# Moving the gate projection's bank evacuation from ScalarE to VectorE, bias included, in a two-block float32 network kernel

## The reference, cut to what matters

```python
h = rms_norm(x, mix_norm)
z = h @ w_in
u, q, k, v, gl = ...                       # pool, attention and gate parts of z
y_pool = multiscale_pool(u, pool_w, pool_scale)
y_attn = moba_attention(rope(norm(q)), rope(norm(k)), v)   # 8 heads, causal softmax
gates = sigmoid(gl + b_gate).reshape(B, S, 2, D)
merged = gates[:, :, 0] * (y_pool @ w_branch_pool) + gates[:, :, 1] * (y_attn @ w_branch_attn)
x = x + merged @ w_out
```

## Time and profile before

| | |
|---|---|
| time, 3 runs | median 1966.62 us (1966.51 to 1966.93) |
| profiled execution: its own time | 1966.62 us |
| its span in the trace | 1964.8 us |
| PE busy | 1953.6 us (99%) |
| DVE busy | 1363.6 us (69%) |
| ACT busy | 1034.5 us (53%) |
| POOL busy | 163.9 us (8%) |
| granted TensorE clock, mean | 0.999 |
| HBM traffic | 183 GB/s over the span |

### The profile page before, as it was taken

How to read it: one execution, slowest core, us unless ns; L and a number is a source line. 1 busy time by engine, 2 the same in 40 slices (tenths; PEclk the granted TensorE clock), 3 DMA queues, 4 the chain that set the end, 5 groups by cost and what they waited for, 6 DMA issues and landing times.

```text
span 1964.8 us, 27601 instructions
## 1 busy us (share of the span) xinstructions
PE 1953.6 (99%) x10534; PEld 1663.7 (85%) x10534; DVE 1363.6 (69%) x1652; ACT 1034.5 (53%) x1201; POOL 163.9 (8%) x152
## 2 busy tenths in 40 slices
PE   9999999999999999999999999999999999999998
PEld 8888978888888889788888978888888978888887
DVE  7666577666676666777666556577888666677887
ACT  6444555544454455655445554356556554456564
POOL 0000130000000003104001201040001301000000
PEclk9999999999999999999999999999999999999999
DMA  8554645455455546456555544564553544555552
GB/s 326 192 183 181 202 142 193 175 189 192 171 193 192 185 159 213 150 180 230 185 190 181 179 174 143 206 249 171 192 192 140 198 177 161 206 211 187 182 187 86
DMA packets 55132, 365.74 MB, mean 186 GB/s; under 512 B 6672, under 2 KB 7952, under 8 KB 12176
## 3 DMA queue, kind: packets, MB, share of 16 engines
q1 hardware_dynamic: 49680, 349.99, 49.9%
q0 software_dynamic: 1472, 9.44, 1.3%
q10 hardware_dynamic: 3904, 5.25, 1.0%
HBM read 359.40 MB, written 1.05 MB: 183 GB/s over the span
## 4 chain that ended last, share of the span: by engine, by line
PE 98%; DVE 1%; ACT 1%; issue 0%; ACTq 0%; POOL 0%; DVEq 0%; POOLq 0%
PE gate_two L1694 13%; PE up_two L1694 12%; PE bank L1624 9%; PE bank L1626 9%; PE bank L1625 9%; PE gate_two L1624 8%; PE gate_two L1626 8%; PE gate_two L1625 8%; PE gate_two L1696 6%; PE up_two L1696 6%; PE bank L1835 1%; PE up_two L1866 1%; PE up_two L1850 1%; PE bank L2127 1%; PE bank L1875 0%; PE gate_two L1636 0%
## 5 line engine op out<-in xcount | busy, mean ns | idle before, releaser
L1019 DVE TENSOR_TENSOR w_lo<-raw,w_hi 128x2048 fp32r<-128x2048 f32 x318 | 736.1, 2316 | 250.2 <-ACT w_hi L569 244.7
L569 ACT ACTIVATE w_hi<-raw 128x2048 fp32r<-128x2048 f32 x322 | 614.3, 1908 | 94.5 <-PE bank L1626 65.8
L1694 PE MATMUL gate_two<-br_parts,w_hi 128*128 128x512 f32 x1056 | 376.5, 399 | 0.1
L1694 PE MATMUL up_two<-br_parts,w_hi 128*128 128x512 f32 x1024 | 364.1, 398 | 0.0
L1696 PE MATMUL gate_two<-br_parts,w_lo 128*128 128x256 f32 x1056 | 296.3, 281 | 0.0
L1696 PE MATMUL up_two<-br_parts,w_lo 128*128 128x256 f32 x1024 | 287.4, 281 | 0.0
L1694 PEld LDWEIGHTS gate_two<-br_parts,w_hi 128*128 128x128 f32 x1056 | 198.4, 188 | 48.8 <-issue 0.8
L1694 PEld LDWEIGHTS up_two<-br_parts,w_hi 128*128 128x128 f32 x1024 | 192.4, 188 | 47.8
L1696 PEld LDWEIGHTS gate_two<-br_parts,w_lo 128*128 128x128 f32 x1056 | 199.4, 189 | 2.3
L1696 PEld LDWEIGHTS up_two<-br_parts,w_lo 128*128 128x128 f32 x1024 | 193.3, 189 | 0.0
L1624 PE MATMUL bank<-w_lo,hid_hi 128*128 128x512 f32 x480 | 188.6, 393 | 0.0
(11 more groups left out here) (274 smaller groups left out, 3010.6 us busy)
## 6 DMA issues: line engine op xcount, KB each, us to landing
raw<-stream SPq DMA_DIRECT2D x328, 1024.0 KB, 4.8
area<-rpb POOLq DMA_DIRECT2D x2, 1536.0 KB, 7.9
area<-rows POOLq DMA_DIRECT2D x3, 1024.0 KB, 5.1
raw<-stream SPq DMA_DIRECT2D x8, 256.0 KB, 7.4
softT<-area ACTq DMA_DIRECT2D x32, 64.0 KB, 5.2
area<-rows POOLq DMA_DIRECT2D x2, 768.0 KB, 4.7
konst<-consts SPq DMA_DIRECT2D x1, 1344.0 KB, 7.7
area<-xT ACTq DMA_DIRECT2D x4, 256.0 KB, 6.8
```

The costliest lines, as they stand in the source:

```text
L569: act.activation(w_hi[:, s, :], raw[:, s, :], ACT.Copy).then_inc(hi_ready[s], 1)
L1019: dve.tensor_tensor(w_lo[:, s, :], raw[:, s, :], w_hi[:, s, :].bitcast(F32), ALU.subtract).then_inc(lo_ready[s], 1)
L1694: pe.matmul(pair[:, f, :, :], w_hi[:, s, at:at + P], parts[:, :, k, :], start=k == 0, stop=False, skip_group_check=True)
```

## The change

ACT no longer empties the gate banks. DVE does it with one `scalar_tensor_tensor` for each bank, `bank * rs + bias row`, eight for each layer (`gated(m, a)`, m = 9, 11, 13, 15). gated(m, 0) is written at the head of DVE's step m, behind a wait for `wide_half`, and gated(m, 1) after the wait for the chunk's end. ACT's eight copies, its waits for `wide_half`, and DVE's four bias instructions are gone, and with them the signals `gate_evac` and `gate_ready`; PE and ACT wait on `mix_scaled` instead, which now counts to 10. The bias rows come in one POOL-issued transfer of 1 MB rather than two. The second edit is on DVE's queue: the `w_lo` split of slot m in steps 7 to 14, which stood in step m + 1 behind that step's scores, is now the last instruction of step m, as in the other steps.

```diff
-                def gate_bias(n):
-                    part = gate_slots[:, 2 * n - 4:2 * n - 2, :] if n >= 2 else merged_tok[:, :, n * 2 * T:(n + 1) * 2 * T]
-                    row = gate_slots[:, n, :] if n < 3 else last_row
-                    dve.wait_ge(gate_rows_in, (layer + 1) * 32)
-                    dve.wait_ge(gate_evac.sem, here.at(gate_evac, 2 * n + 2))
-                    dve.tensor_tensor(part, part, row.unsqueeze(1).broadcast_to([P, TT, 2 * T]), ALU.add
-                                      ).then_inc(gate_ready.sem, 1)
+                def gated(m, a):
+                    gate, half = divmod((m - 9) // 2, 2)
+                    out = gate_slots[:, 2 * half + a, :] if gate else merged_tok[:, a, half * 2 * T:(half + 1) * 2 * T]
+                    dve.scalar_tensor_tensor(out=out, in0=flat(banks[4 + a][:, :, :]), scalar=rs[:, a:a + 1],
+                                             in1=gate_slots[:, (m - 9) // 2, :], op0=ALU.mult, op1=ALU.add
+                                             ).then_inc(mix_scaled.sem, 1)
...
# DVE, loop over m
+                    if m in (9, 11, 13, 15):
+                        dve.wait_ge(gate_rows_in, (layer + 1) * 16)
+                        dve.wait_ge(wide_half.sem, here.at(wide_half, (m - 5) // 2))
+                        gated(m, 0)
...
+                    if m in (9, 11, 13, 15):
+                        gated(m, 1)
...
-                    if 8 <= m < 16:
-                        split_after(here, c - 1)
...
-                    if m in (9, 11, 13, 15):
-                        gate_bias((m - 9) // 2)
-                    if 0 < m < 7 or 15 <= m < MIX1 - 2:
+                    if 0 < m < MIX1 - 2:
                         split_after(here, c)
# ACT, loop over m
-                    if m in (9, 11, 13, 15):
-                        gate_out(m, 1)
...
-                    if m in (8, 10, 12, 14):
-                        act.wait_ge(wide_half.sem, here.at(wide_half, m // 2 - 2))
-                        gate_out(m + 1, 0)
# PE, loop over m
-                    elif m in (10, 12, 14):
-                        pe.wait_ge(gate_evac.sem, here.at(gate_evac, m - 9))
+                    elif 8 <= m < 16:
+                        pe.wait_ge(mix_scaled.sem, here.at(mix_scaled, m - 7))
...
-                                    (lambda: pe.wait_ge(gate_evac.sem, here.at(gate_evac, m - 8))))
+                                    before_second=lambda: pe.wait_ge(mix_scaled.sem, here.at(mix_scaled, m - 6)))
```

More of the change, by code:

```diff
@@ L194, in hybrid_and_neighbourhood_kernel @@
         gate_slots = area3[:, :, :].rearrange("p f t -> p (f t)").rearrange("p (n c) -> p n c", n=HALVES)
-        last_row = area5[:, 6:8, :].rearrange("p f t -> p (f t)")
         gates2_tok, merged_tok = [area[:, :, :].rearrange("p f t -> p (f t)").rearrange("p (a n) -> p a n", a=TT)
@@ L311, in hybrid_and_neighbourhood_kernel @@
         mix_evac = signal("mix_evac", 6, 30)
-        mix_scaled = signal("mix_scaled", 2)
+        mix_scaled = signal("mix_scaled", 10)
         wide_half = signal("wide_half", 5, 9)
@@ L315, in hybrid_and_neighbourhood_kernel @@
         gate_rows_in = sem("gate_rows_in")
-        gate_evac = signal("gate_evac", 2 * HALVES)
-        gate_ready = signal("gate_ready", HALVES)
         branch_evac = signal("branch_evac", 2, 4)
@@ L479, in _ @@
                 pool.wait_ge(qk_ms.sem, here.at(qk_ms, 4))
-                gate_rows = rows1[layer:layer + 1].rearrange("a p n -> (a p) n")
-                pool.dma_start(flat(area3[:, 0:6, :]), gate_rows[:, 0:6 * T]).then_inc(gate_rows_in, 16)
-                pool.dma_start(last_row, gate_rows[:, 6 * T:8 * T]).then_inc(gate_rows_in, 16)
+                pool.dma_start(flat(area3[:, :, :]), rows1[layer:layer + 1].rearrange("a p n -> (a p) n")
+                               ).then_inc(gate_rows_in, 16)
                 pool.wait_ge(konst_in, 16)
@@ L736, in _ @@
                 split_hi(2, here.uses(FFN_CHUNKS + 2))
[L738 to L744, removed]
                 for m in range(MIX1):
@@ L815, in _ @@
                         gates = flat((area2, area3)[m - 15][:, :, :])
-                        act.wait_ge(gate_ready.sem, here.at(gate_ready, 2 * m - 28))
+                        act.wait_ge(mix_scaled.sem, here.at(mix_scaled, 6 + 4 * (m - 15)))
                         for half in range(2):
@@ L1931, in _ @@
                         pe.wait_ge(mix_evac.sem, here.at(mix_evac, m - 1))
-                    elif m == 8:
-                        pe.wait_ge(mix_scaled.sem, here.at(mix_scaled, 1))
-                    elif m in (10, 12, 14):
-                        pe.wait_ge(gate_evac.sem, here.at(gate_evac, m - 9))
+                    elif 8 <= m < 16:
+                        pe.wait_ge(mix_scaled.sem, here.at(mix_scaled, m - 7))
                     elif m == 16:
@@ L1938, in _ @@
                     elif m == 18:
-                        pe.wait_ge(gate_evac.sem, here.at(gate_evac, 8))
+                        pe.wait_ge(mix_scaled.sem, here.at(mix_scaled, 10))
                         pe.wait_ge(att_ready.sem, here.at(att_ready, HALVES))
@@ L1946, in _ @@
                         wide_tokens(c, m % 2, (banks[4], banks[5]), br_hi, br_lo, wide_half,
-                                    before_second=(lambda: pe.wait_ge(mix_scaled.sem, here.at(mix_scaled, 2))) if m == 8 else
-                                    (lambda: pe.wait_ge(gate_evac.sem, here.at(gate_evac, m - 8))))
+                                    before_second=lambda: pe.wait_ge(mix_scaled.sem, here.at(mix_scaled, m - 6)))
                     elif m in (4, 5):
```

## The result

| | before | after |
|---|---|---|
| time, median | 1966.74 us (1966.51 to 1967.97) | 1977.53 us (1974.76 to 1978.88), 5 runs |
| ratio | | 1.0052, 95% interval 1.0038 to 1.0067 |
| span of the profiled execution | 1964.8 us | 1975.9 us |
| granted TensorE clock, mean | 0.999 | 0.998 |

A forecast was written before the change was run, and what follows sets the result against it. PE, busy 1953.6 us, was taken as the bound. First layer 4.3 + 0.3 + 0.5 = 5.1, second 5.0, sum 10.1 us: 1966.62 + 10.1 = 1976.7 us; range 1973.0 to 1980.5, forecast's own 1974.5 to 1979.5.

The forecast's parts named there:

- That PE would wait for DVE at chunks 10, 12 and 14 of each layer: PE's products at these gate chunks wait behind DVE's gate instruction: about 3 to 4 us at 10, 0.3 and 0.5 after.
- not slower: Rival, chance 0.04: freed ACT runs hi(8) ahead, so lo(8) starts by 259 or so and PE never waits; 1966.6 us.
- The chain to chunk 10, without contention: DVE and ACT in one line from lo(7) through gated(9,0): PE waits 3.16 us in the first layer, 3.1 in the second.
- Contention with POOL, +1.1 us in each layer: POOL's sliding sums stretch DVE before chunk 10: +0.5 us for head 1's stat instruction, +0.6 for lo(8).
- the race: lo(7) starts 0.05 us before POOL's instruction and wins the shared ports; were POOL first, 0.6 us more in each layer.
- The second layer's wait: PE's wait before chunk 10 in the second layer: 3.1 us, with POOL's 1.1 it is 4.2.
- The pairs: Chunk 10 to 12 and chunk 12 to 14 in each layer: PE loses 0.3 us, then 0.5 us.
- The loop is closed: DVE does not wait for PE in it: DVE's loop from gated(11,0) to gated(13,0) takes 14.14 us without waiting for PE, against PE's own 13.60.
- The clock, given 0.12: Rival, chance 0.12: the clock falls in the wait before chunk 10, about 2.7 us per slow stretch; 1979.4 to 1982.1 us.
- turn(1) under 1 us: Sign: before chunk 10, PE waits at turn(1) behind the softmax weights for under 1 us, not added to the sum.
- the granted clock leaves 1.00 in the mixing stages: Sign that the forecast is wrong: TensorE's granted clock departs from 1.00 in the mixing stages; no size given.
- What is gained: nothing: Removing ACT's copies, merging the POOL transfer and splitting earlier save zero, as PE waited for none of it.

The follow-up runs named there:

- the repetition: The changed kernel itself, unaltered, run again to compare the others with it on one chip: 1976.5 us, ratio 1.0045.

## Why the prediction was right, and where it was not

- **That PE would wait for DVE at chunks 10, 12 and 14 of each layer: shown.** Six waits in the list, and none when either half of the change is undone, or when the gate instruction stands ahead of lo(8). The forecast's reason for it (both queues in strict order, everything in one line) is what these runs test, and it held. One figure of the rival "not slower" does not come out: "a chain of 8.9 rather than 12.1 us" names no start, and from hi(7) at 253.60 to 264.94 the chain was 11.34. Nothing else uses it.
- **The chain to chunk 10, without contention: right in sum, not in its links.** 9.40 us was worked out and 9.40 measured, twice; in the kernels with added products and in the repetition it is 9.40 or 9.41 in both layers too. Scores to exp was 0.4 too long. It was measured at one head, from the MEMSET at 277.30, and that head's own instructions lie further apart than in other heads, 0.98 us from the first of the scores to the stat instruction in place of 0.67. DVE's timeline of before shows a pause in it; why is not known:

```profile
277.35 0.29 DVE L1161 CUSTOM_DVE_ANT_0 soft<-bank,konst 128x128 f32<-128x128 f32 x1
277.79 0.08 DVE L1161 DVE_READ_ACCUMULATOR2_ANT stat<- 128x1 f32 x1 [0.16 <-issue]
```

- Lo to gated was 0.2 too short (lo(8) took 2.49) and the handover 0.05 should have been about 0.15: the first `gated` takes 0.74 and PE starts 0.88 behind its start. In the sum these cancel.
- **Contention with POOL, +1.1 us in each layer: wrong.** The step that failed took the middle rows of before for the stat instruction and for lo(8). After the change the stat instruction took 0.16 and lo(8) 0.2 more than undisturbed. Both had been stretched by POOL's instructions that stood beside them in the old order; the change moved DVE's instructions against POOL's, so these rows no longer described the neighbours. POOL's timeline beside lo(7) at 256.33:

```profile
256.38 2.82 POOL L489 TENSOR_TENSOR area<-area 128x248 f32<-128x248 f32 x1
```

- Lo(7) began 0.05 us ahead of it, kept its 2.29, and POOL paid: 2.82 for what took 0.72. The turn-taking of the Trainium skill, "SBUF — State Buffer", section "SBUF: two separate sides", agrees in both layers. The prediction had named the race and its outcome, and then added contention further down the chain all the same.
- **The second layer's wait** was shorter, 2.6 against 3.2 us, with the same chain of 9.40: lo(7) started 0.06 us behind chunk 9 there and 0.69 behind it in the first layer, because DVE's first scores began 1.5 us after PE's in the one and 2.7 in the other (1.95 and 2.07 in before). The profiles on record show that this distance varies: 1.2 to 2.7 us over both layers of the ten profiled executions. In the repetition it is 1.36 in the first layer, and lo(7) starts at 254.93, in the changed kernel's first profile at 256.33. The forecast took its start, 255.54, from one execution as if it were fixed. DVE's rows ahead of the scores mostly show it waiting for a DMA (1.51 us in the changed kernel, 0.51 in the repetition), so the DMA's landing is the likely cause; no run tried it. The wait at turn(0), 0.5 us from start to start, is likely of the same origin: it is seen in the first layer alone, and only in the three profiles in which that distance is 2.7 us (the changed kernel, the late splits alone, the gate ahead of the split).
- **The pairs:** 0.3 and 0.5 were forecast, 0.46 and 0.22 measured. DVE's loop from gated(11,0) to gated(13,0) is 13.83 us (14.14 forecast), against PE's 13.60. DVE's rows, then two of ACT's from the loop's second head:

```profile
282.22 1.40 DVE L1208 SCALAR_TENSOR_TENSOR area<-gate_two,rs,area 128x512 f32<-128x512 f32 x2
...
296.05 1.40 DVE L1208 SCALAR_TENSOR_TENSOR area<-gate_two,rs,area 128x512 f32<-128x512 f32 x2
```

```profile
290.57 0.38 ACT L688 ACTIVATE att_hi<-up_two 128x256 fp32r<-128x256 f32 x1
290.83 0.49 ACT L663 ACTIVATE soft<-soft,stat,qk_rs 128x128 f32<-128x128 f32 x1
```

- "The loop is closed: DVE does not wait for PE in it" was wrong. In the loop's first head scores to exp took 0.86, but in its second 1.15: DVE's stat instruction ended at 290.49, and ACT began the exp only at 290.83, since it first took what PE had turned (its row at 290.19 waited 2.78 us for PE). So the path into gated(13,0) runs through PE's own turn at 289.55, and by the rows it is this that makes 0.3 us of the 13.83; with 13.5 the second pair would have had no wait (an estimate from these rows, not tried). The other differences to the forecast are the two gate instructions, 0.1 longer, and the scores-to-exp distance, 0.4 shorter in the first head. That the third pair costs nothing held.
- **The clock, given 0.12: it fell at each of the long gaps that the profiles show.** The price named, 2.7 us for a fall, was too high; it is 1.6. It was taken from the start of the program, which is another stretch. The evidence for this rival was in the prediction (a wait of about the length behind which the clock was seen at 0.50) and was weighed too lightly against a guess that the transposes at the head of the gap would break it. They did not. In the sum of the forecast this is a term put at nothing: 0 in place of 1.6 us in each layer. The Trainium skill, "TensorE: Matmul & The Clock Gate", Part 1, has idleness halve the clock. The traces agree: 0.50 around the end of gaps of 2.40 to 2.54 us.
- **The signs named ahead:** turn(1) under 1 us held in the first layer (0.42; no wait there in the second, nor in the repetition); turn(0), 0.32 in the first layer, had not been named. That DVE would have next to no idle time in its loop was wrong: it waits about 1.2 and 1.1 us for ACT in each head, as the links with ACT in them demand. And "the granted clock leaves 1.00 in the mixing stages" stood there as a sign that the forecast is wrong; by that sign its account of where the time goes was incomplete, though the sum was met.
- **What is gained: nothing.** Held. ACT lost 10 us of work and no wait of PE's became shorter. The new instruction took 0.74 instead of 0.69 on the average of sixteen:

```profile
L1208 DVE SCALAR_TENSOR_TENSOR area<-gate_two,rs,area 128x512 f32<-128x512 f32 x16 | 11.2, 742 | 0.0
```

- In short: waiting was forecast at 10.1 us and came to 7.7 from start to start, and 3.2 us of slow clock made up for it. With the contention left out and the clock counted at 1.6, its own terms would have given 6.3 for the two long waits, 1.6 for the pairs and 3.2 for the clock, 11.1.

## What to carry to other kernels

When an engine's queue gets a new duty that another engine waits for, its place behind or ahead of one long instruction can be the whole cost: here 0.74 us of work was free ahead of the split and cost 9 to 10 us behind it, in a run of links between two engines that nobody had to wait for before. A wait of TensorE's that is priced by its length alone is priced too low: ask what the clock does behind it, and count some products after the gap at the slower spacing as a case of its own, since one profile does not tell how often it happens. And a duration that another engine's work had stretched belongs to the old timing of both; after a move, look up anew who stands beside whom, or bound the contention rather than add it.

## What the runs showed of the hardware

- The granted clock fell at gaps of PE of 2.40 to 2.54 us, in each of the five that were seen (two in the changed kernel, two in its repetition, one with products in the first layer only), and not at the 1.23 and 1.48 us of the kernel with two added products. Between these no gap was tried at this place. At another place it fell once in ten profiles behind 1.69 us, so these lengths are no rule.
- When it fell varied. In the changed kernel it was 1.00 when the products began again at 265.73 and fell 1.3 us later, and 0.5 us after 799.00 in the second layer; with products in the first layer only, 0.8 us after 796.14; in the repetition 0.65 us after 264.33, but 0.3 us before the products began again at 797.75, still in the gap. It stayed at 0.50 for 3.4 us each time, and came back while PE was working. The products were 0.43 us apart in place of 0.22 to 0.23. Eight of them at 0.2 more make the 1.6 us.
- Two small products in the gap, 1.13 us in the timeline, kept the clock there as five did.
- DVE's handover to PE behind the gate instruction is about 0.15 us, while ACT's to DVE at the split and DVE's to ACT at the exponential were 0.03 to 0.04.
